# Two halves of a bank: hi and lo as one 512-wide moving operand in the 256-token stages

## What is computed

```
x = x + 0.5*ml[2] * swiglu(modulate(rms_norm(x, g1), ml[0], ml[1]), ffn1_w_in, ffn1_w_out)   # and cx
hx, hc = modulate(rms_norm(x, g2), ...), modulate(rms_norm(cx, g2), ...)
bg, cg, vc, q, k, v, gt = split(hx @ w_in)
y = conv_branch(bg, cg, vc, conv_w)              # bg * conv(cg * vc)
o = attention(rope(norm(q)), [k_c, k_l], [v_c, v_l])
x = x + ml[5] * ((sig(gt0) * (y @ w_bc) + sig(gt1) * (o @ w_ba)) @ w_out)
x = x + 0.5*ml[8] * swiglu(modulate(rms_norm(x, g3), ...), ffn2_w_in, ffn2_w_out)
x = rms_norm(x, final_g)
...
h = rms_norm(x, norm_mix)                        # second block
x = x + (ga * (nsa_attention(h) @ w_ba) + gb * (pool_mixer(h) @ w_bp)) @ w_out
x = x + square(relu(rms_norm(x, norm_mlp) @ w_ff1)) @ w_ff2
out = rms_norm(x, norm_final)
```

## Time and profile before

| | |
|---|---|
| median of 3 runs | 1351.22 us (1348.61 to 1351.72) |
| the profiled execution's own time | 1352.08 us |
| its span in the profile | 1350.3 us |
| mean granted TensorE clock | 0.973 |
| PE / weight loads / DVE / ACT / POOL busy | 96% / 85% / 54% / 44% / 4% |
| matmuls | 8912 |
| DMA | 214 MB, 159 GB/s |

### The profile page before, as it was taken

How to read it: one execution, slowest core, us unless ns; L and a number is a source line. 1 busy time by engine, 2 the same in 40 slices (tenths; PEclk the granted TensorE clock), 3 DMA queues, 4 the chain that set the end, 5 groups by cost and what they waited for, 6 DMA issues and landing times.

```text
span 1350.3 us, 23476 instructions
## 1 busy us (share of the span) xinstructions
PE 1295.4 (96%) x8912; PEld 1150.9 (85%) x8912; DVE 728.5 (54%) x1217; ACT 590.5 (44%) x885; POOL 59.6 (4%) x72
## 2 busy tenths in 40 slices
PE   5899999999999999999998999998999998999997
PEld 3677777778887799889998999997798888999997
DVE  2533333333333765776665555556467765756664
ACT  2443123422233446544445556545345564544542
POOL 1000000000001000000001000002013101000001
PEclk7899999999999999999998999997999999899998
DMA  9544444444224334423453554543532224455542
GB/s 390 214 186 154 172 175 187 170 174 185 87 71 157 116 134 160 152 94 116 165 189 121 222 199 172 189 161 117 187 125 94 94 98 151 156 187 187 186 161 88
DMA packets 30956, 214.13 MB, mean 159 GB/s; under 512 B 3376, under 2 KB 4656, under 8 KB 5936
## 3 DMA queue, kind: packets, MB, share of 16 engines
q1 hardware_dynamic: 30032, 209.73, 42.4%
q10 hardware_dynamic: 864, 3.56, 0.7%
HBM read 212.23 MB, written 1.05 MB: 158 GB/s over the span
## 4 chain that ended last, share of the span: by engine, by line
PE 86%; DVE 6%; ACT 4%; DMA 2%; issue 2%; DVEq 0%; ACTq 0%; SPq 0%
PE ps_u L1433 25%; PE ps_u L1434 25%; PE ps_u L1435 25%; PE ps_a L1408 2%; ACT w_hi L475 1%; PE ps_a L1391 1%; PE ps_a L1380 1%; DMA scr<-in_mods 1%; DMA raw<-in_stream 1%; DVE w_lo L815 1%; PE ps_a L1646 1%; DVE sq L871 1%; PE ps_a L1583 1%; PE ps_a L1568 1%; PE ps_a L1397 1%
## 5 line engine op out<-in xcount | busy, mean ns | idle before, releaser
L1433 PE MATMUL ps_u<-x_hi,w_hi 128*128 128x256 f32 (+1 forms) x1744 | 547.6, 314 | 19.5 <-DVE x_lo L882 10.5
L815 DVE TENSOR_TENSOR w_lo<-raw,w_hi 128x1024 fp32r<-128x1024 f32 x322 | 394.6, 1229 | 291.8 <-ACT w_hi L475 287.3
L1434 PE MATMUL ps_u<-x_lo,w_hi 128*128 128x256 f32 (+1 forms) x1744 | 539.6, 309 | 0.0
L1435 PE MATMUL ps_u<-x_hi,w_lo 128*128 128x256 f32 (+1 forms) x1744 | 538.9, 309 | 0.0
L475 ACT ACTIVATE w_hi<-raw 128x1024 fp32r<-128x1024 f32 x322 | 337.8, 1054 | 308.0 <-PE ps_u L1435 267.8
L1433 PEld LDWEIGHTS ps_u<-x_hi,w_hi 128*128 128x128 f32 x1744 | 337.8, 194 | 49.7 <-issue 28.8
L1435 PEld LDWEIGHTS ps_u<-x_hi,w_lo 128*128 128x128 f32 x1744 | 337.7, 194 | 15.7
L1434 PEld LDWEIGHTS ps_u<-x_lo,w_hi 128*128 128x128 f32 x1744 | 338.0, 194 | 15.1 <-issue 0.5
L1433 PE MATMUL ps_u<-h_hi,w_hi 128*128 128x256 f32 (+1 forms) x800 | 246.2, 308 | 0.5 <-DVE h_lo L956 0.5
L1434 PE MATMUL ps_u<-h_lo,w_hi 128*128 128x256 f32 (+1 forms) x800 | 245.2, 307 | 0.0
L1435 PE MATMUL ps_u<-h_hi,w_lo 128*128 128x256 f32 (+1 forms) x800 | 245.1, 306 | 0.0
(11 more groups left out here) (225 smaller groups left out, 806.4 us busy)
## 6 DMA issues: line engine op xcount, KB each, us to landing
raw<-in_stream SPq DMA_DIRECT2D x153, 1024.0 KB, 4.8
wide_scr<-in_mods SPq DMA_DIRECT2D x18, 1024.0 KB, 6.7
scr<-in_mods SPq DMA_DIRECT2D x18, 1024.0 KB, 6.8
raw<-in_stream SPq DMA_DIRECT2D x8, 768.0 KB, 4.1
x<-in_tokens ACTq DMA_DIRECT2D x2, 1024.0 KB, 14.6
wide_scr<-in_cmp_w SPq DMA_DIRECT2D x2, 1024.0 KB, 7.9
sq<-in_cmp_w SPq DMA_DIRECT2D x2, 1024.0 KB, 8.6
out<-x SPq DMA_DIRECT2D x4, 256.0 KB, 2.3
```

The lines of the kernel that those rows point to most:

```text
L815: dve.tensor_tensor(w_lo[:, k % 2, cols], raw[:, k % 2, cols], w_hi[:, k % 2, cols].bitcast(F32), ALU.subtract).then_inc(l_ready, 1)
L1433: pe.matmul(dst, wh, xh, start=(kc == 0), stop=False)
L1434: pe.matmul(dst, wh, xl, start=False, stop=False)
L1435: ins = pe.matmul(dst, wl, xh, start=False, stop=(kc == span - 1))
```

## The change

x_hi and x_lo become the two halves of one tile `x_hl` (128 x 2 x 8 x 512), h_hi and h_lo those of `h_hl`. In a 256-token unit PE multiplies w_hi with both at once: one matmul of 2 x 256 columns whose output is a whole PSUM bank, the hi product in columns 0 to 255 and the lo product in 256 to 511. w_lo times x_hi still goes to the first half. So hi and lo come out in two halves of a bank that have to be added. ACT copies the second halves of both banks to SBUF (`copy_lo`), then DVE adds the first halves to them (`add_hi`), and the stage's own work follows on SBUF operands. Out units add both halves onto `x` in two passes with a semaphore between.

```
-                        pe.matmul(dst, wh, xh, start=(kc == 0), stop=False)
...
+                        both = operand(kc, t)
+                        xh, xl = both[:, 0, :], both[:, 1, :]
+                        if wide:
+                            halves = ps_u[:, 2 * b + t, :].rearrange("p (a n) -> p a n", a=2)
...
+                                pe.matmul(halves, wh, both, start=(kc == 0), stop=False)
+                                ins = pe.matmul(dst, wl, xh, start=False, stop=False)
...
+            def copy_lo(k, dst):
+                act.activation(dst, ps_u[:, 2 * (k % 2):2 * (k % 2) + 2, S:NB], ACT.Copy).then_inc(lo_copied, 1)
...
+            def add_hi(k, dst, copies):
+                dve.wait_ge(lo_copied, copies)
+                return dve.tensor_tensor(dst, ps_u[:, 2 * (k % 2):2 * (k % 2) + 2, 0:S], dst, ALU.add)
```

In a swiglu's in unit ACT's part becomes:

```
+                                pair = lo_rows(k + j)
+                                copy_lo(k + j, pair)
+                                act.wait_ge(summed, c - count + 2 * p + (SUMS["ffn2"] + j + 1))
+                                act.activation(pair[:, 0, :], pair[:, 0, :], ACT.Silu).then_inc(silu_done, 1)
```

An out unit on DVE goes over `x` twice:

```
+                for part in range(1 if terms is None else 2):
+                    if part:
+                        ins.then_inc(out_terms, 1)
+                        dve.wait_ge(out_terms, terms)
```

More of the change, by code:

```diff
@@ L97 @@
 LANDED = 16
+LO_COPIES = {"q": 0, "gates": 4, "conv": 12, "bg": 20, "merge": 24, "ffn2": 32, "ksvs": 54, "pool": 56, "gates2": 58, "ff": 66}
+SUMS = {"gates": 0, "conv": 8, "bg": 16, "merge": 20, "ffn2": 28, "ff": 50}
 def program(nc, a, out):
@@ L113, in program @@
         x = sb("x", [P, KD, NB])
[L114 to L117, removed]
+        x_hl = sb("x_hl", [P, 2, KD, NB], F32R)
+        h_hl = sb("h_hl", [P, 2, KD, NB], F32R)
         sq = sb("sq", [P, KD, NB])
@@ L158, in program @@
         ps_a = ctx.enter_context(nc.psum_tensor("ps_a", [P, 4, 512], F32))
+        x_hi, x_lo = x_hl[:, 0, :, :], x_hl[:, 1, :, :]
+        h_hi, h_lo = h_hl[:, 0, :, :], h_hl[:, 1, :, :]
         sq_flat = sq[:].rearrange("p k n -> p (k n)")
@@ L610, in _ @@
             act.activation(root[:, 16:32], ps_a[:, 1, 16:32], ACT.Sqrt, bias=eps, scale=1.0 / HD).then_inc(qroot_done, 1)
-            with act.Fori(1, 4) as p:
+            for p in range(1, 4):
                 gates(p)
@@ L703, in _ @@
                 split(0, k + 5 + g, 1)
-            splits(0, k + 7)
-            splits(0, k + 8)
+            for i in range(2):
+                split(0, k + 7 + i, 0)
+                done(0, k + 5 + i)
+                copy_lo(k + 5 + i, pooled[:, 2 * i:2 * i + 2, :])
+                split(0, k + 7 + i, 1)
             def turned_probs(h):
@@ L1415, in riding, with unit @@
                 mod(u, 1 if c == N_MOD - 1 else (c - 2) % 3 if c < N_MOD - 2 else 0, u % MOD_QUARTERS, n % 4, LANDED * (n // 4 + 3), c - 1)
[L1417 to L1420 removed]
+            def unit(pr, k, operand, n=S, kcs=KD, ready=None, parts=1, wide=True):
+                pe.wait_ge(drained, 2 * pr + (k + 1))
+                b = k % 2
+                wide = wide and n == S and parts == 1
                 span = kcs // parts
@@ L1456, in swiglu, with slab @@
             def swiglu(base, i, n):
-                def slab(s, pr, k, chunks):
+                def slab(s, pr, k, chunks, last=False):
                     with pe.Fori(0, chunks // 2) as p:
@@ L1613, in _ @@
                     unit(p, FIRST["merge"] + j, both_h, ready=branches_ready)
-            with pe.Fori(0, 2) as p:
-                for j in range(2):
-                    unit(p, FIRST["wout"] + j, from_x(S), ready=drained_at(0, FIRST["merge"]))
+            for o in range(4):
+                unit(0, FIRST["wout"] + o, from_x(S), ready=drained_at(0, FIRST["merge"]), wide=o < 3)
             stat(2, 2)
@@ L1793, in _ @@
                         unit(s * 4 + p, FIRST["ff"] + 4 + j, from_h(S), ready=drained_at(s * 4, FIRST["ff"], 2))
+            ff_last = 4 * (SLABS2 - 1)
+            ff_ins(ff_last)
+            for o in range(4):
+                unit(ff_last, FIRST["ff"] + 4 + o, from_h(S), ready=drained_at(ff_last, FIRST["ff"], 2), wide=o < 3)
             stat(5, 2)
```

239 lines of the change are left out of this document (134 added, 105 removed).

## The result

| | before | changed |
|---|---|---|
| median (runs) | 1351.08 us (4, 1348.61 to 1351.72) | 1359.24 us (4, 1358.21 to 1361.5) |
| ratio | | 1.0065, 95% interval 1.0050 to 1.0081 |
| span of the profiled execution | 1350.3 us | 1356.4 us |
| matmuls | 8912 | 7100 |
| granted TensorE clock, mean | 0.973 | 0.980 |

The change makes the kernel 0.65% slower, 8.2 us. The forecast was 1362 (1340 to 1377), slower with 0.62.

What follows compares the result with a forecast made beforehand. The prediction took PE, busy 96% of the span, to bound the kernel, with evictions as critical in parts. Its terms, -22.8 + 18.3 + 6.0 + 5.5 + 3.5 = +10.5 us, gave 1362 us, range 1340 to 1377.

Steps and rivals of the forecast that it cites:

- I take the measured spacings to add: PE's wide units: a 512 and a 256 pass take 227.4 + 120.0 = 347.4 ns, saving 12.6 a pair, 22.8 us.
- Rival (c): Wide units on PE: the wide pass takes 240 ns and saves nothing, up to 15 us more, 1377 us; chance 0.12.
- conv, 6.0 forecast: Conv heads: u_pad comes 1.0 to 1.1 us later, PE's transposes wait for h_lo in seven heads; 6.0 us lost.
- ffn2, 18.3 forecast: ffn2: losses of 5.1 in slab one, 6.8 in two, 2.4 in three, 4.0 in the last four out units.
- The ring: ffn2's slabs of eight: weight landing to landing for two units goes from 12.44 to 13.1 us, against PE's 11.12.
- Slab two starts with the landing at about the unit's end: ffn2's slab two: landing no longer 4.0 us ahead, so two units take 13.1 instead of 11.1; loss 6.8 us.
- bg, merge, wout, 5.5 forecast: These stages: 3.8 us of PE waits, plus 0.6 and 1.1 at stages' first units; 5.5 us lost.
- If the landing is late the ring is 12.2: Merge: with a late weight landing, two units' round of splits, eviction and DMA takes 12.2 us, over PE's 11.1.
- bg leaves none: bg, weights' round 12.0 us, starts with plenty of slack and leaves none, so merge's eight units run at the round's pace.
- ff, 3.5 forecast: ff's four slabs: the last in unit's h_lo is late for chunk 6, 0.75 us each, first worse by 0.5; 3.5 lost.
- Rival (a): Whole kernel: the deadlines hold, only ffn2's first slab still waits, for 5.1 us; 1334 us; chance 0.17.
- rival (b): Whole kernel: half the waits, ffn2 slabs as forecast but merge, tail and chunk waits absent, some 16 us lost; 1345; chance 0.15.

Runs made afterwards that it cites:

- evict_first: Half of w_lo's split moved behind add and product on DVE in bg, merge and ff, against both_fixed; 1337.82 us, ratio 0.9902 to the kernel before.
- both_fixed: Changed kernel with conv's h_lo ahead of the convolution, ffn2's ACT loops written out and ffn2's last four out units narrow; 1340.11 us, ratio 0.9933.

## Why the prediction was right

The direction, the size and the mechanism held: +10.5 forecast, +8.1 by the trace, +8.2 by the medians. Both sides of the sum were too large, the saving by 4.6 us and the losses by 7.0, and the errors partly cancelled: that the total came within 2.4 us is in part luck.

*The saving, 22.8 forecast, 18.2 by the measured pace of a pair.* The step that was off is "I take the measured spacings to add": 227.4 + 120.0 = 347.4 ns. In the mix a pair takes 350.0: units alternate between 5.56 us (347.5 a pair, as forecast) and 5.64 (352.5), see below. Rival (c), that the wide pass saves nothing, is out: alone it brings 17 us.

By the N/2.4 + 2.5 ns of the Trainium skill, "TensorE: Matmul & The Clock Gate", section "Back-to-back issue gap", the pair would have saved 2.5 ns, an estimate from the page's figure. The section calls this the gap of isolated matmuls, and for a stream with weight loads it has some 131 ns at N = 512; this case's trace has 227.4. The saving in the trace is 10.0 ns a pair, so here the measurement decides: with a weight load for every matmul (8912 of both before) one matmul less was worth four times the 2.5 ns. Why is not shown.

*conv, 6.0 forecast, 7.7 measured.* The wait is at the place and on the tile that was named, h_lo for PE's transposes. A head's weighted sum and h_lo lie 0.9 further apart, where 0.95 to 1.05 was forecast. With the 0.16 that each unit saves, six of the seven heads lost 0.4 to 1.0 each (0.5 to 1.05 forecast), but between the second and the third PE lost 2.6 (13.13 us in place of 10.71), which I had not seen coming: that head's wait for h_lo is the longest of the seven, 2.9 us. With h_lo moved the step is 10.73 again. That it is the order and not the amount of work was shown by moving one operation.

*ffn2, 18.3 forecast, 12.7 measured.* The ring was forecast at 13.1 and is 12.95; the pairs of units at 13.1 and are 12.8 to 12.9. What failed is "Slab two starts with the landing at about the unit's end": the first landing of slab two came at 812.77, 1.6 us ahead of the end of its first unit (814.39). So the pair of units after the first ones lost only 1.1 us (12.2 us from 820.04 to 832.28) and two pairs ran at the ring's pace, not three. ACT, that landing and the next:

```profile
812.77 1.28 ACT L480 ACT_TABLE_LOAD   x1 [2.67 <-DMA raw<-in_stream]
...
825.76 1.28 ACT L480 ACT_TABLE_LOAD   x1 [0.94 <-DMA raw<-in_stream]
```

With the late chunk of the first out unit, lost were 3.5 in slab one (5.1 forecast), 4.9 in slab two (6.8), 0.5 in slab three (2.4) and 3.7 in the tail, all of it in its last two units (4.0). In slab one, too, a late unit less came than forecast: its first four units still ran 0.3 us faster than before. The term of slab three had next to nothing behind it, one wait of 0.22 us for h_lo.

*bg, merge, wout, 5.5 forecast, 1.4 measured.* The step "If the landing is late the ring is 12.2" is right (merge's last landings are 12.0 apart), but "bg leaves none" is wrong: PE waited first at merge's sixth unit, after five without a wait. The last three units of merge took 5.94, 5.80 and 6.05 and wout's first 6.78, some 2.1 us of waits; the loss is smaller than that because wout's last unit and the norm behind it took 12.74 in place of 13.46. That is not the change's doing: the granted clock fell from 2.4 to 1.2 GHz 8.0 us after this unit's start before, and 10.0 us after it now.

*ff, 3.5 forecast, 3.4 measured*, 2.8 of it before chunk 6 as forecast: 1.6 in the first slab, 0.3 to 0.5 in each of the others (0.75 forecast).

*gates2, 0 forecast.* The changed kernel has no wait for h_lo there, but by luck: in the kernels whose clock stayed up in the first head PE waits 1.2 to 1.4 us for it in the second (see "Evictions ahead of w_lo").

Rival (a) is out, with 7.7 us lost in conv alone; rival (b), half the waits, was the nearest: three quarters of what I summed up in bg, merge and wout and a third of it in ffn2 stayed away, but the saving was smaller too.

## What to carry to other kernels

A cheaper form on the busiest engine is worth its saving only if what it hands on is ready in the same time: here the pass alone brings 17 us and the longer eviction alone costs 22. Before such a change, read from the timelines how late each eviction may be, and afterwards look at the order on the evicting engine first: one operation moved ahead of a convolution, a loop written out, the last four out units left narrow and w_lo put into a gap gave back everything and 12 us more (1337.8 against 1350.3). Compare such repairs with the kernel before as well: of the 9 us that the written-out loop gave, 3 were there without the change.

## What the runs showed of the hardware that I had not expected

Wide units alternate between 5.64 and 5.56 us with an otherwise steady stream, in each kernel that has them. After a wait the phase can turn (ff's 14th unit takes 5.64 and the 22nd, in the same slot and banks, 5.56), so it is tied neither to the slot nor to the banks. The narrow stream has no such beat: 5.76 each time. The distance of the two rows doesn't change it. Its cause is open.

ACT's table loads stood in the hardware loops of ffn2's slabs of eight, two for each two units (at the loop's first ACTIVATE and ahead of silu), 16 in all; with the loops written out one is left (871 ACT instructions in place of 886).

The last out unit of ffn2 and its norm show what the granted clock can do to one execution. With the same code in ffn2 it fell from 2.4 to 1.2 GHz 7.0 us after that unit's start in evict_first and 9.7 us after it in both_fixed, and the 24 matmuls with one moving column took 5.28 and 3.93 us. In both, PE had finished the stream of the unit and then waited 2.9 us for ACT's squares; the clock fell within that wait in the first and 2.4 us behind it in the second. When to expect the fall, these runs don't show.
